# Sums of squares as two rounded passes over split squares, and row maxima turned in one rounded pass

## What is computed

```python
q = (c_q @ w_q_b).reshape(B, L, N_HEADS, QK_HEAD_DIM)            # 8 heads, 96 = 64 + 32 wide
kv = (c_kv @ w_kv_b).reshape(B, L, N_HEADS, QK_NOPE_DIM + V_HEAD_DIM)
k_nope, v = kv[..., :QK_NOPE_DIM], kv[..., QK_NOPE_DIM:]
k = jnp.concatenate([k_nope, k_pe], axis=-1)
q, k = rmsnorm_2(q, g_qn), rmsnorm_2(k, g_kn)                    # x * rsqrt(mean(x * x) + eps) * gain
...                                                              # rotary embedding of the last 32
s = einsum(q, k) * scale                                         # causal, 1040 positions
p = softmax(s)                                                   # exp(s - row maximum) / sum
o = p @ v
```

## Time and profile before

| | |
|---|---|
| time before, median of 3 | 3325.3 us (3324.19 to 3326.75) |
| the profiled execution, own time | 3325.28 us |
| its span | 3323.5 us |
| TensorE busy | 3054.6 us, 92% |
| VectorE busy | 1412.9 us, 43% |
| ScalarE busy | 697.2 us, 21% |
| GpSimd busy | 1068.6 us, 32% |

### The profile page before, as it was taken

The page is one execution under the profiler, slowest core; times in us unless marked ns, Lnnn a source line. Parts: engine busy times, 40 slices in busy tenths (PEclk is TensorE's granted clock), DMA queues, the critical chain, the costliest instruction groups (busy, mean ns, idle before and its releaser), DMA issues.

```text
span 3323.5 us, 41150 instructions
## 1 busy us (share of the span) xinstructions
PE 3054.6 (92%) x16352; PEld 2687.3 (81%) x16352; DVE 1412.9 (43%) x1726; ACT 697.2 (21%) x1241; POOL 1068.6 (32%) x1335
## 2 busy tenths in 40 slices
PE   6986687899999997799999899999899999899999
PEld 4764565777778775799999788889899999788889
DVE  4658454422222223820011666671820111666671
ACT  2142321000000002100111455510100111455510
POOL 3523013444444443333333211133433432211132
PEclk9997788999999998899999999999999999999999
DMA  2111011111111111211212100051211212000052
GB/s 105 44 32 35 1 70 37 47 50 44 44 50 44 44 50 38 82 47 45 96 51 78 38 14 14 14 181 51 90 51 45 97 46 83 33 14 14 14 187 77
DMA packets 46429, 182.50 MB, mean 55 GB/s; under 512 B 5968, under 2 KB 6096, under 8 KB 45776
## 3 DMA queue, kind: packets, MB, share of 16 engines
q1 hardware_dynamic: 31248, 113.19, 10.9%
q10 hardware_dynamic: 15040, 67.28, 5.3%
HBM read 150.06 MB, written 30.39 MB: 54 GB/s over the span
## 4 chain that ended last, share of the span: by engine, by line
PE 83%; DVE 12%; ACT 3%; issue 1%; DMA 0%; DVEq 0%; ACTq 0%; SPq 0%
PE acc L425 62%; PE acc L726 4%; PE aux L842 4%; PE acc L821 3%; DVE act_lo L1440 2%; PE acc L775 2%; PE acc L710 2%; DVE work L1456 1%; DVE work L1449 1%; DVE act_hi L1439 1%; PE acc L796 1%; DVE residual L1505 1%; PE acc L738 1%; PE acc L748 1%; PE acc L520 1%
## 5 line engine op out<-in xcount | busy, mean ns | idle before, releaser
L425 PE MATMUL acc<-act_hi,w_hi 128*128 128x348 f32 (+1 forms) x3104 | 768.7, 348 | 71.3 <-DVE act_lo L1440 36.0
L353 POOL TENSOR_TENSOR w_lo<-w_raw,w_hi 128x256 fp32r<-128x256 f32 (+1 forms) x924 | 810.4, 910 | 17.3
L425 PE MATMUL acc<-act_lo,w_hi 128*128 128x348 f32 (+1 forms) x3104 | 763.1, 346 | 0.0
L425 PEld LDWEIGHTS acc<-act_hi,w_hi 128*128 128x128 f32 x3104 | 545.2, 190 | 131.1 <-issue 52.6
L425 PE MATMUL acc<-act_hi,w_lo 128*128 128x348 f32 (+1 forms) x3104 | 616.7, 344 | 0.0
L425 PEld LDWEIGHTS acc<-act_lo,w_hi 128*128 128x128 f32 x3104 | 548.1, 190 | 43.3
L425 PEld LDWEIGHTS acc<-act_hi,w_lo 128*128 128x128 f32 x3104 | 527.7, 189 | 42.4
L373 POOL TENSOR_TENSOR small<-shape_consts 128x1 f32<-128x1 f32 x192 | 42.8, 223 | 1574.6 <-PE acc L425 1574.6
L425 PE MATMUL acc<-ff_split,w_hi 128*128 128x512 f32 (+1 forms) x1408 | 317.7, 375 | 12.0 <-DVE ff_split L1440 12.0
L1655 DVE TENSOR_TENSOR residual<-acc,residual 128x1024 f32<-128x1024 f32 (+1 forms) x88 | 108.1, 1228 | 460.0 <-PE acc L425 460.0
L425 PEld LDWEIGHTS acc<-ff_split,w_hi 128*128 128x128 f32 x1408 | 252.9, 188 | 61.0 <-DVE ff_split L1440 16.6
(11 more groups left out here) (228 smaller groups left out, 3288.4 us busy)
## 6 DMA issues: line engine op xcount, KB each, us to landing
w_raw<-in_wstream SPq DMA_DIRECT2D x215, 512.0 KB, 3.5
spill_x<-residual ACTq DMA_DIRECT2D x2, 4176.0 KB, 12.2
spill_m<-residual ACTq DMA_DIRECT2D x2, 4176.0 KB, 12.5
spill_g<-work ACTq DMA_DIRECT2D x16, 522.0 KB, 2.7
residual<-spill_m ACTq DMA_DIRECT2D x16, 522.0 KB, 6.1
work<-spill_g ACTq DMA_DIRECT2D x16, 522.0 KB, 8.9
residual<-spill_x ACTq DMA_DIRECT2D x16, 522.0 KB, 4.4
residual<-in_xT ACTq DMA_DIRECT2D x8, 512.0 KB, 9.8
```

The source lines that it names most:

```text
L353: ins = nc.gpsimd.tensor_tensor(Wl[:, s, c0:c0 + w], Wraw[:, s, c0:c0 + w], Wh[:, s, c0:c0 + w].bitcast(F32), ALU.subtract)
L425: ins = nc.tensor.matmul(acc[0:m, s, p, 0:w], wt[:, ws, w0 + j * m:w0 + j * m + m], x[:, k, p * w:p * w + w], start=(first and t == 0), st ...
```

## The change

- The squares of keys and queries are written twice by ScalarE, once in f32 and once rounded (`key_hi`, `query_hi`). VectorE subtracts the two into a rounded low part (`key_lo`, `query_lo`). `key_sum` and `query_sum` become two rounded passes, over the high and the low part, with a rounded matrix of ones. They wait for VectorE's subtraction (`k_square_split`, `q_square_split`) instead of ScalarE's square.
- The maxima go to columns of a rounded tile `row_max`, 34 columns for each 128 rows with the maximum in column 32 and zeros elsewhere. `turn_maxima` multiplies such 34 columns with the rounded identity in one pass.
- VectorE fills the rounded ones, the lower 64 rows of `key_hi` and `key_lo` and the zeros of `row_max` ahead of the loop.
- The ring of probabilities has five slots, which makes room in `pool_split`.

```diff
-        PRING = 6
+        PRING = 5
...
+        row_max = G_[:, idr0 + 3 * P:idr0 + 3 * P + 34 * TB]
+        extra0 = idr0 + 3 * P + 34 * TB
+        split0 = extra0 + QP
+        key_hi, key_lo = (G_[:, split0 + TP * i:split0 + TP * i + TP] for i in range(2))
+        query_hi, query_lo = (G_[:, split0 + 2 * TP + QP * i:split0 + 2 * TP + QP * i + QP] for i in range(2))
+        ones96_r = G_[:, split0 + 2 * TP + 2 * QP:split0 + 2 * TP + 2 * QP + P]
...
-                    pe.wait_ge(sems["k_squared"], k)
-                    nc.tensor.matmul(acc_n[:, 0:w], ones96, X[:, 6, c0:c0 + w], start=True,
-                                     stop=True).then_inc(sems["k_sum"], 1)
+                    pe.wait_ge(sems["k_square_split"], k + l + 1)
+                    for part in (key_hi, key_lo):
+                        ins = nc.tensor.matmul(acc_n[:, 0:w], ones96_r, part[:, c0:c0 + w], start=part is key_hi,
+                                               stop=part is key_lo)
+                    ins.then_inc(sems["k_sum"], 1)
...
-                    pe.wait_ge(sems["q_squared"], k)
-                    nc.tensor.matmul(acc_n[:, 0:w], ones96, qsq[k % 2][:, 0:w], start=True,
-                                     stop=True).then_inc(sems["q_sum"], 1)
+                    pe.wait_ge(sems["q_square_split"], k)
+                    for part in (query_hi, query_lo):
+                        ins = nc.tensor.matmul(acc_n[:, 0:w], ones96_r, part[:, 0:w], start=part is query_hi,
+                                               stop=part is query_lo)
+                    ins.then_inc(sems["q_sum"], 1)
...
-                        ins = nc.tensor.matmul(acc_r[bank][32:33, o:o + n], S_[:, 16 + i:17 + i], ident[:, P - n:P],
+                        ins = nc.tensor.matmul(acc_r[bank][0:34, o:o + n], row_max[:, 34 * i:34 * i + 34], ident_r[:, P - n:P],
...
-                    do(nc.scalar.activation(X[top, 6, c0:c0 + w], acc_n[top, 0:w], ACT.Square), "k_squared")
+                    do(nc.scalar.activation(X[top, 6, c0:c0 + w], acc_n[top, 0:w], ACT.Square))
+                    do(nc.scalar.activation(key_hi[top, c0:c0 + w], acc_n[top, 0:w], ACT.Square), "k_squared")
...
-                    do(nc.scalar.activation(qsq[k % 2][:, 0:w], acc_q[:, 0:w], ACT.Square), "q_squared")
+                    do(nc.scalar.activation(qsq[k % 2][:, 0:w], acc_q[:, 0:w], ACT.Square))
+                    if k > 1:
+                        act.wait_ge(sems["q_sum"], k - 1)
+                    do(nc.scalar.activation(query_hi[:, 0:w], acc_q[:, 0:w], ACT.Square), "q_squared")
...
+                def key_square_split(g, pc):
...
+                    dve.wait_ge(sems["k_squared"], k)
+                    do(vec.tensor_tensor(key_lo[top, cols], X[top, 6, cols], key_hi[top, cols].bitcast(F32),
+                                         ALU.subtract), "k_square_split")
+
+                def query_square_split(g, pc):
...
+                    dve.wait_ge(sems["q_squared"], k)
+                    do(vec.tensor_tensor(query_lo[:, 0:w], qsq[k % 2][:, 0:w], query_hi[:, 0:w].bitcast(F32),
+                                         ALU.subtract), "q_square_split")
...
-                    dve.wait_ge(sems["q_squared"], k)
+                    query_square_split(g, pc)
...
+                    to = row_max[:, 34 * i + 32:34 * i + 33] if i < 4 else S_[:, col:col + 1]
+                    do(vec.tensor_reduce(to, acc_r[rough_bank(i, p)][:, 0:n], AX, ALU.max, negate=True), "rough_max")
...
+                do(vec.tensor_copy(ones96_r, ones96))
+                do(vec.tensor_copy(key_hi[0:64, :], X[0:64, 6, :]))
+                do(vec.tensor_tensor(key_lo[0:64, :], X[0:64, 6, :], key_hi[0:64, :].bitcast(F32), ALU.subtract),
+                   "k_square_split")
...
+                do(vec.tensor_scalar(row_max, C_[:, 0:34 * TB], 0.0, None, ALU.mult))
...
+                        if more and n in (1, 6, 11):
+                            key_square_split(g, n // 5)
```

## The result

| | before | changed |
|---|---|---|
| median | 3325.64 us (5 runs) | 3402.91 us (3400.90 to 3405.84, 5 runs) |
| span of the profiled execution | 3323.5 us | 3401.6 us |
| TensorE busy | 3054.6 us, 92% | 3045.8 us, 90% |
| VectorE busy | 1412.9 us | 1466.8 us |
| ScalarE busy | 697.2 us | 730.3 us |

The ratio is 1.0235 with a 95% interval of 1.0223 to 1.0248. The kernel is slower by 77 us, where 43 were forecast: the sign is right, the size lies outside the range, and the missing 35 us are what the experiments had to find.

What follows compares the result with a forecast made beforehand. TensorE was taken as the bound, a VectorE chain right beside it. Per head 2.65 us saved, 0.74 of old waits gone and 5.7 of new waits gave +2.3; two layers added 42.6, so 3368 us, range 3344 to 3390.

Steps and rivals of the forecast that it cites:

- What bounds the kernel: Steady heads: TensorE, busy 40.09 of 40.82 us, with two old waits of 0.40 and 0.34 and a VectorE chain beside it.
- TensorE's saving: Cheaper sums save 1.58 us a head and cheaper turns of the maxima 1.07, together 2.65 us.
- Step 9 and step 14: Query sums wait for VectorE's subtraction, queued behind the rough maximum: new waits of 1.49 and 1.76 us.
- Steps 7 and 12: Rough scores wait for rounded queries, as VectorE's chain gets two more links: net +0.57 and +0.24 us.
- Step 4's wait: Query sum waits some 0.15 us for the subtraction behind the last maximum; net -0.14 with the cheaper sum.
- Sum of a head: Steady head: 2.65 us saved, 0.74 of old waits gone, 5.7 of new waits, in all +2.3 us.
- Head -1: Preparation of the first head: VectorE's constants and first split delay the first key sum; in all +6.4 us.
- the sum of a layer: First head's preparation 6.4, seven heads at 2.3 and -1.2 for the last: 21.3 us, two layers 42.6.
- rival (d): TensorE's clock falls to its lower level for one head in each layer: 3390 to 3440 us, chance 0.03.
- The ring of five: Probability ring: five slots cost nothing, since ScalarE's free slot holds values weighed two steps earlier in TensorE's order.
- Rival (b): Subtractions come in time for the query sums of steps 9 and 14: head -1.4 us, time 3315, chance 0.08.
- head 7: Last head of a layer, preparing nothing: two cheaper turns and a shorter VectorE chain, -1.2 us.

Runs made afterwards that it cites:

- e_border: Kernel before the change with only the VectorE and ScalarE instructions reordered where that applies, sums and turns still f32: 3316.8 us.
- e_turn: Changed kernel with f32 squares and sums taken back, keeping only the rounded turn of the maxima and five ring slots: 3316.6 us.
- e_fill: Changed kernel plus 10 and 14 needless rounded products on TensorE in the waits before the query sums of steps 9 and 14: 3371.7 us.
- e_fill_all: Changed kernel with needless products before the query sums of steps 4, 9 and 14 and each layer's first key sum: 3365.5 us.
- e_sums: Changed kernel with the maxima turned in f32 again, keeping the sums over split squares and five ring slots: 3403.6 us.
- e_ring5: Kernel before the change with five probability ring slots instead of six, nothing else: 3324.4 us, ratio 1.0001.
- e_early: Changed kernel with VectorE's query-square subtraction moved ahead of the rough maximum in steps 9 and 14 only: 3339.2 us.
- e_best: Changed kernel with VectorE and ScalarE instructions reordered, and only the constants the first key sum needs ahead of the loop: 3302.5 us.

## Why the prediction was right in its sign and wrong in its size

**What bounds the kernel**: right. e_border takes the two old waits away and a head gets shorter by 0.5 us (not 0.7, since a new wait of 0.56 appears); a VectorE chain does stand right beside TensorE.

**TensorE's saving**: right for the sums. The turn was put at 0.34 us with 34 columns, by the nearest rows with 128; it takes 0.18 (1988.51 to 1988.69 in e_turn), and 0.14 where the third product has 20 columns (1952.48 to 1952.62 above). The rule of the Trainium skill, "TensorE: Matmul & The Clock Gate", section "LDWEIGHTS (loading the stationary operand)", by which a load follows its columns and the turn was estimated at 0.16, was nearer than the row; the load of 34 columns is recorded at about 110 ns, that of 128 at about 188, so the records do not shrink in proportion. The prediction's objection to it, that six one-column loads and their passes still take 0.74, was a misreading: one f32 sum over as many columns, 384, takes 0.64 already, which leaves 0.10 for all of its loads.

**Step 9 and step 14**: right in place and cause. From rough scores to sum 1.62 us were measured and 1.55 forecast in step 9, and 2.05 and 1.82 in step 14. Most of the surplus of step 14 is VectorE's subtraction, 0.66 instead of 0.45, while GpSimd was busy with the weights of the next head (3.80 of 4.00 us in the window above); that the one slows the other is not shown here.

**Steps 7 and 12**: right; 0.92 and 1.41 us waited, 0.84 and 0.99 forecast (1994.65 - 1993.66). VectorE's chain has the length that was forecast (6.38 us from the sum to the rough scores of step 12, 6.40 forecast); TensorE comes earlier, 0.16 of it by the turn at 0.18, and waits for the same chain. Step 4's wait was small, as forecast; in step 5 the last rough scores start 0.36 behind the mask product (1995.53 and 1995.89) where it was 0.06, so the wait there is 0.30 instead of 0.47.

**Sum of a head**: close. In e_fill and e_fill_all the heads take 43.2 us at a clock of 1.00, on average 2.5 more than before where 2.3 were summed. **Head -1 and the sum of a layer**: e_fill_all gives +5.9 and +5.8 us for head -1 (6.4 forecast) and a time of 3365.5 (3368). From the first projection to the last weighing a layer of it takes 362.4 and 364.5 us, before 340.9 and 343.0: +21.5 each, 21.3 forecast. That it agrees so closely is in part luck: the turns saved more than was summed and the waits were longer, and the steady heads came out above their forecast and head -1 and head 7 below.

**The step that failed is rival (d).** It held that the clock would stay at 1.00 in the steady heads since TensorE would be busy in the same share as in 1865 to 1880, 13.02 of 15 us, 0.87. The share came out as reckoned, 39.07 of 44.84, also 0.87, and the clock fell all the same, beside the wait of step 14, in every head. The mean over the head was the wrong thing to read. In that stretch of the kernel before no wait was longer than this one, of its TensorE timeline:

```profile
1874.20 0.48 PE L775 MATMUL acc<-ff_split 128*128 128x512 f32 x1 [1.18 <-issue]
```

In the changed kernel TensorE was idle 1.8 of the 4 us before the fall. The Trainium skill, "TensorE: Matmul & The Clock Gate", "Part 1: The HAM clock gate", says that the clock falls after idleness of TensorE; the trace agrees in kind, with 1.82 us of wait and the two L715 rows at 0.32 behind it, though TensorE had worked in more than half of those 4 us. And the rival was priced wrongly, as an event of a whole head with a chance of 0.03, where it is a tax of 1.9 us on the average head and of 9 us on the two heads -1. The sign of being wrong that the prediction gave for it, a granted clock under 1 in the heads, came: 0.96. The term "clock" belonged into the sum: 37 us. What decides whether a wait of this size is followed by a fall is not shown: in e_sums 4 of 14 were not.

**The ring of five** costs nothing: right, by e_ring5. **Rival (b)**, that the subtractions might be in time, was rightly denied for the order as written, and e_early and e_best show that it was the order alone that denied it. Its time was too low: e_early, which is that case, came out at 3339, not 3315. Its heads take as long as before instead of 1.4 us less, since VectorE's chains of steps 7 and 12 bind once the sums are in time, and its two heads -1 lose 15 us instead of 10.

## What to carry to other kernels

A cheaper instruction on the bounding engine that needs a new product of another engine is worth nothing until it is clear where that product stands in the other engine's order; here two instructions a head, moved ahead of a maximum, decided over 64 of the 77 us. When waits are added to TensorE, price its clock with them: look at the longest wait and the microseconds around it, not at the share of a whole stage. Where a wait cannot be removed, and only where the engine would idle anyway and nothing is delayed, needless products in a free bank can be cheaper than the low clock.

## What the runs showed of the hardware

- Adding work to TensorE made a kernel faster by 31 us (e_fill) and 37 us (e_fill_all): a granted clock of 0.96 in a head became 1.00 (e_fill).
- The granted clock fell from 1.00 to 0.57 in the 4 us behind 4 us in which TensorE was busy 2.18 us, in a head in which it was busy 87% of the time, and was back at 1.00 in the next 4. Behind 4 us with 2.11 us busy, in e_sums, it stayed at 1.00.
- Three rounded products with 34 columns of weights and 128 columns of data hold TensorE for 0.18 us (e_turn, 1988.51 to 1988.69); with 128 columns of weights it was 0.34.
